# Stores of the expert gates shared by two DMA queues, and a third row buffer in the projection of tiles 1 to 3, in a hybrid encoder layer

## The reference

```python
q = rms_norm((hf @ w_query).reshape(t, PEER_HEADS, 2 * PEER_KEY_DIM))
...
top_score, top_pos = lax.top_k(cand_score, PEER_TOPK)
expert_idx = jnp.take_along_axis(cand_idx, top_pos, axis=-1)
gate = jax.nn.softmax(top_score, axis=-1)
...
u_sel = jnp.take(expert_u, idx, axis=0)
act = jax.nn.gelu(jnp.einsum('tkd,td->tk', u_sel, hb).astype(jnp.float32), approximate=False) * gb
v_sel = jnp.take(expert_v, idx, axis=0)
return jnp.einsum('tk,tkd->td', act.astype(hb.dtype), v_sel)
```

## Time and profile before

| | us |
|---|---|
| median of 3 runs | 3222.39 |
| the three runs | 3218.49 to 3225.63 |
| profiled execution | 3213.22 |
| its span | 3211.5 |
| PE busy | 2930.1 (91%) |
| DVE busy | 2181.7 (68%) |
| POOL busy | 1536.5 (48%) |
| ACT busy | 1177.6 (37%) |

### The profile page before, as it was taken

How to read it: one execution, slowest core, us unless ns; L and a number is a source line. 1 busy time by engine, 2 the same in 40 slices (tenths; PEclk the granted TensorE clock), 3 DMA queues, 4 the chain that set the end, 5 groups by cost and what they waited for, 6 DMA issues and landing times.

```text
span 3211.5 us, 43156 instructions
## 1 busy us (share of the span) xinstructions
PE 2930.1 (91%) x17829; PEld 2756.9 (86%) x17829; DVE 2181.7 (68%) x3093; ACT 1177.6 (37%) x1389; POOL 1536.5 (48%) x630
## 2 busy tenths in 40 slices
PE   6899898876598999999888889999999999999998
PEld 5677787654487999999888889999999999999998
DVE  5756466655477659999767566666676666667666
ACT  6755532315423233334233333333333333333331
POOL 0000353312133337864234367777776666666662
PEclk9899999987799999999989999999999999999999
DMA  7747547854478776665877898998989898888985
GB/s 302 263 157 276 195 161 297 296 214 154 161 305 323 293 277 227 226 237 202 273 257 253 300 358 336 345 339 344 345 336 365 347 354 341 344 346 345 354 343 214
DMA packets 189564, 915.75 MB, mean 285 GB/s; under 512 B 16944, under 2 KB 76448, under 8 KB 86464
## 3 DMA queue, kind: packets, MB, share of 16 engines
q1 hardware_dynamic: 81680, 475.30, 40.5%
q0 software_dynamic: 56112, 406.05, 32.4%
q10 hardware_dynamic: 51648, 32.77, 3.2%
HBM read 872.31 MB, written 41.68 MB: 285 GB/s over the span
## 4 chain that ended last, share of the span: by engine, by line
PE 63%; DMA 16%; DVE 12%; ACT 4%; ACTq 2%; issue 2%; POOL 1%; SPq 0%; DVEq 0%; POOLq 0%
PE ps L1538 8%; PE ps L1847 7%; PE ps L1849 7%; PE ps L1848 7%; PE ps L1778 7%; DMA rows<-peer_u_rows,idx_far 7%; PE ps L1779 7%; PE ps L1780 7%; DMA g_in<-gelu_scratch 5%; PE ps L1763 4%; PE ps L1525 3%; DVE rows L1241 3%; PE ps L1821 2%; ACTq L953 2%; DVE ps L1251 2%
## 5 line engine op out<-in xcount | busy, mean ns | idle before, releaser
L545 POOL TENSOR_TENSOR ring_lo<-ring_raw,ring_hi 128x2048 fp32r<-128x2048 f32 x217 | 1029.6, 4747 | 855.0 <-ACT ring_hi L618 853.7
L618 ACT ACTIVATE ring_hi<-ring_raw 128x2048 fp32r<-128x2048 f32 x400 | 763.3, 1915 | 650.5 <-DMA ring_raw<-w_in 221.3
L1778 PE MATMUL ps<-bT_hi,ring_hi 128*128 128x320 f32 x2048 | 647.9, 316 | 49.0 <-ACT ahead L930 43.1
L1847 PE MATMUL ps<-a_hi,ring_hi 128*128 128x320 f32 x2048 | 637.6, 311 | 26.9 <-DVE a_lo L1388 25.2
L1779 PE MATMUL ps<-bT_lo,ring_hi 128*128 128x320 f32 x2048 | 639.9, 312 | 0.0
L1780 PE MATMUL ps<-bT_hi,ring_lo 128*128 128x320 f32 x2048 | 639.6, 312 | 0.0
L1848 PE MATMUL ps<-a_lo,ring_hi 128*128 128x320 f32 x2048 | 634.1, 310 | 0.0
L1849 PE MATMUL ps<-a_hi,ring_lo 128*128 128x320 f32 x2048 | 633.9, 310 | 0.0
L1028 DVE TENSOR_TENSOR ring_lo<-ring_raw,ring_hi 128x2048 fp32r<-128x2048 f32 x183 | 426.6, 2342 | 258.5 <-ACT ring_hi L618 258.4
L571 POOL DMA_INDIRECT rows<-peer_u_rows,idx_far x128 | 215.7, 1685 | 515.7 <-DVE z_far L1241 498.5
L1778 PEld LDWEIGHTS ps<-bT_hi,ring_hi 128*128 128x128 f32 x2048 | 391.6, 191 | 51.0 <-ACT ahead L930 44.4
(11 more groups left out here) (289 smaller groups left out, 3845.2 us busy)
## 6 DMA issues: line engine op xcount, KB each, us to landing
ring_raw<-peer_u SPq DMA_DIRECT2D x128, 1024.0 KB, 5.2
ring_raw<-peer_v SPq DMA_DIRECT2D x128, 1024.0 KB, 5.6
ring_raw<-w_in SPq DMA_DIRECT2D x80, 1024.0 KB, 4.9
ring_raw<-w_out SPq DMA_DIRECT2D x32, 1024.0 KB, 4.9
ring_raw<-w_query SPq DMA_DIRECT2D x32, 1024.0 KB, 5.5
gates_scratch<-gbuf ACTq DMA_DIRECT2D x20, 1024.0 KB, 12.2
g_pair<-gates_scratch SPq DMA_DIRECT2D x64, 320.0 KB, 7.9
gelu_scratch<-ahead ACTq DMA_DIRECT2D x72, 160.0 KB, 5.2
```

What stands on the lines that cost most here:

```text
L545: pool.tensor_tensor(ring_lo[s][:], ring_raw[s][:], ring_hi[s][:].bitcast(F32), ALU.subtract)\
L618: act.activation(ring_hi[place(n)][:], ring_raw[place(n)][:], ACT.Copy).then_inc(hi_ok[SLOT[n]], 1)
L1778: pe.matmul(dst, hi[:, e], bT_hi[:, k, 0:NEAR], start=(k == 0), stop=False)
L1847: pe.matmul(dst, hi[:, col], a_hi[:, par, e, :], start=(e == 0), stop=False)
```

## The change

Five things are changed. (1) In pieces 92 to 104 a third buffer, `rows_4`, at 144 KB, serves the rows; ACT writes the U part of the projection there only once the last row that uses it is done. (2) In pieces 93 to 111 DVE makes the low half of piece n + 1 between the rows of piece n, instead of that of piece n ahead of them. (3) There are fewer rows early on: one instead of two in every fourth piece from 94 to 110, 14 instead of 20 in the attention (4, 4, 4 and 2 in its four turns instead of 5 each), one less in piece 126 and none in 127. 13 rows more stand in pieces 284 to 395. (4) The low halves of pieces 112 and 113 are made in the first turn of the attention. (5) Of the four stores of a batch SP issues two, behind its load of the piece four past the batch's last; ACT issues one behind the copies and one a block later.

```diff
@@ rows and their buffers
-ATTEND_ROWS = 20
+ATTEND_ROWS = (4, 4, 4, 2)
...
+BATCH_END = [HOT_FIRST + len(HOT_BATCH) * _b + 3 for _b in range(BATCHES)]
...
     for n in range(92, OUT_B):
-        ROWS_AT[n] = 2
-    ROWS_AT[OUT_B - 1] += ATTEND_ROWS
+        ROWS_AT[n] = 1 if n % 4 == 2 else 2
+    ROWS_AT[OUT_B - 1] += sum(ATTEND_ROWS)
     for n in range(OUT_B, AHEAD - 1):
-        ROWS_AT[n] = 1 if n % 4 == 3 and n < QUERY_B else 2
+        ROWS_AT[n] = 0 if n == QUERY_B - 1 else 1 if n == QUERY_B - 2 or n % 4 == 3 and n < QUERY_B else 2
...
-        have = [0, 1] + ([2] if ROW_POS[r] >= OUT_B else []) + ([3] if r >= P else [])
+        have = [0, 1] + ([4] if ROW_POS[r] <= 104 else []) + ([2] if ROW_POS[r] >= OUT_B else []) + ([3] if r >= P else [])
@@ SP
+            for b in range(BATCHES):
+                load_upto(AHEAD + BATCH_END[b] + 4)
+                sp_eng.wait_ge(g_out, 16 * (b + 1))
+                for g in range(G_PARTS // 2):
+                    sp_eng.dma_start(*gate_part(b, g)).then_inc(g_stored, 16)
             load_upto(DOWN - 2)
@@ POOL, gather
+                elif b == 4:
+                    pool.wait_ge(x1_stored, 16)
@@ ACT, evac_b and the expert pieces up
+                    act.wait_ge(row_used, 1 + max(r for r in range(N_ROWS) if ROW_BUF[r] == 4))
...
-                if HOT_AT[i] and jj % 16 == 0:
+                if i in BATCH_END:
                     act.wait_ge(g_out, jj)
-                    for g in range(G_PARTS):
-                        store_gates(jj // 16 - 1, g)
+                    act.dma_start(*gate_part(jj // 16 - 1, 2)).then_inc(g_stored, 16)
+                elif i - 1 in BATCH_END:
+                    act.dma_start(*gate_part(jj // 16 - 1, 3)).then_inc(g_stored, 16)
@@ DVE
+            lo_upto(92)
             for n in range(92, OUT_B):
-                lo_upto(n)
-                rows_step(ROWS_AT[n] - (ATTEND_ROWS if n == OUT_B - 1 else 0))
+                count = ROWS_AT[n] - (sum(ATTEND_ROWS) if n == OUT_B - 1 else 0)
+                rows_step(1)
+                lo_upto(min(n + 1, OUT_B - 1))
+                rows_step(count - 1)
...
-                rows_step(ATTEND_ROWS // (HEADS // 2) - 2)
+                if i == 0:
+                    lo_upto(OUT_B + 1)
+                rows_step(ATTEND_ROWS[i] - 2)
```

More of the change, by code:

```diff
@@ L246, in layer @@
     g_in = [at("g_in_0", [P, NEAR], F32, 154.5), at("g_in_1", [P, NEAR], F32, 190.5)]
-    rows = [at(f"rows_{b}", [P, D], F32, kb) for b, kb in enumerate((164, 172, 156, 180))]
+    rows = [at(f"rows_{b}", [P, D], F32, kb) for b, kb in enumerate((164, 172, 156, 180, 144))]
     x_end = [at(f"x_end_{t}", [P, D], F32, 48 + 8 * t) for t in range(4)]
@@ L347, in layer @@
         d_made, y_added = sem("down_done"), sem("expert_y_added")
-        gathered = [sem(f"gathered_{b}") for b in range(4)]
+        gathered = [sem(f"gathered_{b}") for b in range(5)]
         row_used, far_gelu, far_weight = sem("row_used"), sem("far_gelu"), sem("far_weight")
@@ L360, in wait_piece, with gate_part @@
             eng.wait_ge(freed[SLOT[n]], USE[n])
+        def gate_part(b, g):
+            n = NK // 2 // G_PARTS
+            return (gates.rearrange("h j b i t -> j h b (i t)")[:, g * n:(g + 1) * n, b, :],
+                    gbuf[:].rearrange("p (h i) t -> p h (i t)", i=2)[:, g * n:(g + 1) * n, :])
         def bcast(ap, shape, *axes):
@@ L947, in copy_gates @@
                    .then_inc(g_out, 1)
-            def store_gates(b, g):
-                n = NK // 2 // G_PARTS
-                dst = gates.rearrange("h j b i t -> j h b (i t)")[:, g * n:(g + 1) * n, b, :]
-                src = gbuf[:].rearrange("p (h i) t -> p h (i t)", i=2)[:, g * n:(g + 1) * n, :]
-                act.dma_start(dst, src).then_inc(g_stored, 16)
             def gelu_to_psum(i, bank):
```

## The result

| | us |
|---|---|
| changed kernel, median of 4 runs | 3147.3 (3142.57 to 3153.75) |
| kernel before, median of 4 runs on the same chip | 3220.44 (3217.72 to 3225.63) |
| ratio, with its 95% interval | 0.9758 (0.9735 to 0.9781) |
| profiled execution after, and its span | 3142.57, 3140.8 |

What follows compares the result with a forecast made beforehand. Taken as mostly matmul on PE (63% of the span), with only PE's waits to gain: 41.6 + 23.6 + 5.2 + 32 = 102.4 us off the profiled 3213.2, near 3111; forecast 3120 us, range 3095 to 3156.

Steps and rivals of the forecast that it cites:

- stores land too late: Rival in batches: fourth store lands late, next batch's copy and PE wait; gain 66 us, 3156 us, chance 0.13.
- three signs of being wrong: First ACT copy of a batch waits for stores; load behind SP's stores too late for PE; last expert stage slows.
- Projection: Pieces 92 to 111: third buffer and fewer rows give PE's pace to piece 104; 41.6 of 48.6 lost us gained.
- stay lost: Projection from piece 105: two buffers left, 56 us where PE wants 49, so 7 us remain lost.
- Attention: Fewer rows: shorter DVE waits for gathers, ACT's root no longer held up, low halves moved; 23.6 us gained.
- End of the output projection: Three rows less, so low half 129 and the additions come earlier; 5.2 us gained, bounds 3 and 5.2.
- Batches: Stores split between SP and ACT: 9 us gained in each of four, 4 lost in the first; 32 us gained.
- 20 us of queue time are spread over 30: Argument that a batch's stores, issued over a longer time, would not land as much later as they are issued.
- The rule cited: DMAs of several engines share 16 engines; spreading saves only issuing time, so a batch's last store lands no sooner.
- the forecast loss: First batch: row 125's gather behind two low halves delays hot columns; 12 us waiting, 2.5 at lower clock.
- Last stage: Last expert stage takes 13 more rows; DVE has room, PE waits for nothing: 0 us, bound 39 us lost.
- the last stage pays: Rival: the 13 moved rows cost the last expert stage up to half of 39 us; 3140 us, chance 0.10.

Runs made afterwards that it cites:

- low_first: Changed kernel with DVE's low half of piece n back ahead of that piece's rows in the projection; 3141.53 us, ratio 0.9743.
- stores_only: Kernel before with only the batches' stores changed, as split between SP and ACT in the change; 3201.78 us, ratio 0.9949.
- three_on_sp: Changed kernel with three stores of a batch on SP and one on ACT behind the copies; 3146.18 us, ratio 0.9770.
- no_batch_rows: Changed kernel with all rows taken out of the batches' pieces and moved to later ones; 3146.51 us in one run.
- lag_one: Changed kernel with POOL issuing the gather of row 125, second row of piece 186, one low half earlier; 3136.74 us, ratio 0.9729.
- all_pool: Changed kernel with POOL making all low halves of the last stage, including DVE's 28 of 112; 3144.89 us, ratio 0.9748.
- skip_13: Changed kernel without the last 13 gathered rows of the second expert table, output share missing; 3136.13 us, ratio 0.9711.
- buffer_only: Kernel before with only the third row buffer and its two waits added; 3202.29 us, ratio 0.9932.

## Why the prediction was right, and where it was wrong

The forecast was 3120 us and the kernel takes 3147.3, inside the range of 3095 to 3156, whose upper end is the price of the rival "stores land too late". Of its 102 us 73 came, and 12.9 of the 70 in the table (pieces 131 to 184) are ones that it didn't have: without them the time would be near 3160, past the range. Of its three signs of being wrong two came, a copy that waits for the stores and a last stage that slows down, and the third, a load that comes too late behind SP's stores, is part of the first. So two of its parts are right as mechanisms, one is badly sized, and one is wrong.

**Projection: right.** 43.2 us for 41.6. The mechanism (a buffer's release to its next landing, 11.0 us for two rows) holds in three kernels: on two buffers 33 rows take 180.7 us, and a third buffer lifts the pace to PE's. Of the forecast 7 us that "stay lost" in the two-buffer stretch 5.4 did, and the chain above has the gathers there from 585 us on. But `low_first` has the same two buffers in that stretch and lost nothing (163.2 us), so this size is met in one kernel and not in the other.

**Attention: right,** 21.6 for 23.6 (`stores_only`, with the attention of the kernel before, took 200.0 us and not 195.8), and ACT's wait ahead of the root is gone as said. **End of the output projection:** 3.4 for 5.2, within the bounds.

**Batches: mis-sized, 32 forecast, 0.9 measured from load 184 to 288.** The step that failed is "PE's 8.36 us go ... I take 2 us lost in a batch, 9 gained". PE's wait for the GELU went, but the later batches' period fell from 67.9 to 64.5, 3.4 us and not 9. The rival "stores land too late" named the place: the copies come late, and PE waits for them for 5.0 us in each of four batches, plus the lower clock behind. The argument against it ("20 us of queue time are spread over 30") was the mistake. The queues' time isn't spread: the stores were all issued within 6.5 us (12.6 in the second batch), and beside them run the loads, since PE goes on. The stores took 25 us to land instead of 20. The load behind them, of which the forecast said "some 4 us later", was issued 6.4 us past the first store in both kernels and landed 22.2 us past it instead of 14.0 (third batch). The kernel before moved 20.3 us x 316 GB/s = 6.4 MB behind a batch, with PE standing still for 8.4 us of it; the changed one moves 25.3 x 331 = 8.4 MB at the same share of 1.02 to 1.03. Taking the issuing away thus only let PE run on until the copies stopped it. The rule cited, of the Trainium skill's "DMA: Bandwidth & Descriptors", section "Issuing engines are not separate DMA queues", had it right: the last store lands no sooner (24.6 to 27.6 us past the first one's issue, 20.2 to 20.8 before). `three_on_sp` shows that the stores are only one of two things that the copy stands behind: with its stores landing 4 to 6 us sooner the load comes 0.7 us later, and the period of its undisturbed later batches is 63 us still. That it is the sum of bytes which sets the 25 us is argued from the share of 1.03 in either order. `no_batch_rows` is no test of it, since without the gathers still 25.0 x 309 = 7.7 MB are moved, at a share of 0.98; its copy comes after the same 25.0 us, so bytes alone don't explain it. No kernel took away loads or stores alone, and stores in longer packets weren't tried either.

In the first batch the forecast loss was named rightly (row 125, the hot columns: 34.3 us behind the last copy for 35.4 forecast) and is in size 11 us, the period of 75.8 against 64.5 in the others, which `no_batch_rows` takes away. It was forecast as 12 of waiting and 2.5 of clock, all for the hot columns. But PE waits only 3.2 us for them, and 5.8 for a low half behind: it is not one wait, and with the gather issued earlier the copy takes its place (`lag_one`). Where the remaining 5.4 us between load 215 and 288 went was narrowed to that load behind SP's wait, and is within the scatter.

**Last stage: wrong, 0 forecast and 11.3 us lost.** The step was "DVE is busy for 528 of 787 us there and has room for 13 x 2.35 = 31". By busy time it has. But a low half of DVE that doesn't start ahead of POOL's has to wait for it, and 13 more rows brought that about for 7 of 28 instead of 1: 27 us more of DVE, right in front of PE's piece. The forecast's bound of 39 us and the rival "the last stage pays" reckoned with bytes; the loss was in their range for another reason. The 12 us that the prediction works out for a ceiling of the bandwidth meet the measured 11.3 by chance, since `all_pool` moves the same bytes in 783.6 us. `all_pool` takes back 9.2 of the 11.3 us and `skip_13` 6.7; each keeps one wait for a low half of POOL (1.9 and 2.9 us), and for the rest no cause is shown. The Trainium skill, "SBUF — State Buffer", section "Who interferes with whom", states that a VectorE instruction with both inputs in SBUF contends with a GpSimd instruction that reads SBUF, and that the order of issue decides which of them blocks the other. The trace agrees, with 6.93 us as 4.65 + 2.28 where POOL won and POOL's 5.74 where DVE did. From some 0.3 us apart on whoever started first by the record won; DVE lost all four times that it was 0.11 or 0.12 us ahead, so starts that close in the record don't tell.

**Pieces 147 to 184: 8.5 us gained that the forecast didn't have.** PE's waits there fell from 6.4 us for DVE's selB plus 4.0 for a sum to 2.5. DVE's comparisons ahead of selB, of before and after (count | busy, mean ns), of which another six fell from a mean of 4174 to 3292 ns:

```profile
L1196 DVE TENSOR_TENSOR eqB<-eqB,i12fB 128x2048 f32<-128x2048 f32 x6 | 29.2, 4859 | 0.1
```

```profile
L1208 DVE TENSOR_TENSOR eqB<-eqB,i12fB 128x2048 f32<-128x2048 f32 x6 | 26.7, 4447 | 0.1
```

The likely reading is that they met POOL's low halves less often: the same collision, with the other sign, by chance. That stage takes 266 us in every kernel with the changed rows and 275 in `stores_only` and `buffer_only`, so the rows' places make it. The rest is argued, and not everything there got shorter: three operations of `gate_eB` rose from a mean of 3243 to 4722 ns.

What runs beside the stores could have been added up beforehand; the collision could be foreseen only as a risk, since tenths of a microsecond decide it.

## What to carry to other kernels

A stall in issuing stores can hide another limit right behind it: before giving the gain to a second queue, add up the bytes that will move in the freed time, and ask who next waits for the stores and who for the loads issued behind them. Where two engines make alike pieces with two inputs in SBUF, count room not by busy time but by which of the two starts first, and expect any move of other work to change that. And a loss that is forecast rightly at one instruction can still stand in front of another of the same size, so that only removing both tells.

## What the runs showed of the hardware that was not expected

- An SBUF-to-SBUF subtraction of 128x2048 on DVE takes 2.28 us, and 6.4 to 6.9 when POOL's (4.65 us) starts a little ahead or up to 0.12 us behind; 0.41 us ahead of POOL's it takes its 2.28 and POOL's 6.37; rows' operations that take one input from PSUM keep their 2279 and 2348 ns in the same stage. The reduction with both inputs in SBUF had a mean of 3892 ns in pieces 147 to 184, the one with an input in PSUM 2279 in the last stage (count | busy, mean ns | idle before), which the port that POOL shares would explain:

```profile
L1253 DVE CUSTOM_DVE_ANT_0 rows<-rows,h_far 128x2048 f32<-128x2048 f32 x16 | 62.3, 3892 | 11.0 <-DMA rows<-peer_u_rows,idx_far 10.5
```

```profile
L1253 DVE CUSTOM_DVE_ANT_0 rows<-rows,ps 128x2048 f32<-128x2048 f32 x64 | 144.6, 2279 | 1.3 <-DMA rows<-peer_u_rows,idx 1.3
```

- The stores of 1 MB, four to a batch, took 9.1 to 24.3 us each from issue to landing on two queues with the loads beside them (median 16.1 of all 20), on one queue with PE held up 6.8 to 14.0 (median 12.2), from the views of the gate buffer's tile:

```profile
DMA to landing us min/median/max: 9.1/16.1/24.3
```

```profile
DMA to landing us min/median/max: 6.8/12.2/14.0
```

- The DMA queues carried 362 GB/s over 800 us in `all_pool`, more than the 358 that the Trainium skill's "DMA: Bandwidth & Descriptors", section "Specifications", gives as a core's limit for HBM, and PE kept its pace. Only one core ran here.
